# The expert layers of a two-layer encoder step: rows of the first two experts gathered by a 0/1 product, ranks in four products, weight slots reassigned, expert rows moved to other queues

## The chip, the cores and the metric

One core of one Trainium2 chip. The metric is the device time of one execution in microseconds (us). TensorE does matmuls, VectorE (DVE) and ScalarE (ACT) elementwise work, GpSimd (POOL) mostly issues DMAs here, SyncE (SP) only issues DMAs. Each engine runs its own instruction list in order and meets the others at semaphores. All DMA queues are served by the core's 16 DMA engines.

## The reference

Two layers over 384 tokens (256 of a prompt, 128 of eight samples), each with a mixer and a mixture of experts. Layer 0 mixes with a chunked gated MLP, layer 1 with latent attention. The part that the change touches is the mixture of experts and what stands right before and after it:

```python
t = xn.reshape(-1, D_MODEL)                    # 384 x 1024, after an RMS norm
lg = tf @ w_group + b_group                    # 4 groups, top 1
le = (tf @ w_expert + b_expert)                # 16 experts, 4 in a group
top_v, top_i = lax.top_k(le_sel, 2)            # top 2 in the chosen group
wts = softmax(top_v) * g_p
for e in range(16):                            # only the routed tokens count
    hdn = silu(t @ w1[e]) * (t @ w3[e])        # 1024 -> 512
    y = y + gates[:, e:e+1] * (hdn @ w2[e])    # 512 -> 1024
```

## The kernel before, in words

All products with large weights are done in three passes of the reduced-precision float type: the weight is split on ACT into a high part (`moe_split_h`, line 1028) and on DVE into the rest (`moe_split_l`, line 1032), and x likewise. One expert weight is 2 MB and has the number j = 0 to 47 in a layer: j = 0, 1 are w1 and w3 of expert 0, 2 and 3 those of expert 1, 4 is w2 of expert 0, 5 is w1 of expert 2, and from there w1[e] is 3e-1, w3[e] is 3e and w2[e] is 3e+4 (the last w2 is 47). TensorE does product j from bank to bank in this order and counts `w_used`. "Product j" below is the 24 matmuls of 512 columns of one weight (lines 181 and 187).

Six slots hold raw weights, six the low parts, three the high ones (w_hi). Six weights are loaded ahead of the loop, and load j waits until product j-6 is done. In layer 0 the slots 2 to 5 are free before the output product of the gated MLP ends, the slots 0 and 1 only near its end; before the change expert 0's w1 and w3 sit in slots 0 and 1.

Routing of a layer (`route_tensor`, `route_scalar`, `route_vector`): the mixer's last product ends; DVE adds it to h and multiplies by the gain for each of three row tiles (lines 378 and 878 in layer 0, 1483 and 878 in layer 1); TensorE transposes each tile (line 996), ACT copies it, TensorE computes the logits (line 1003). ACT takes the square root of the mean squares, DVE scales the rows (885) and then does a chain of small operations, each waiting for the last: logits (889), group, two experts per token, the matrix `picked` of 0 and 1. TensorE ranks the tokens of each expert with nine products against a triangle and a block of ones (1016). DVE turns ranks into destination rows (910 to 927). POOL scatters the normed rows to `moe_xrows` in DRAM, six indirect DMAs (849). When they have landed, SP loads the 72 rows of experts 0 and 1 (744), TensorE transposes them (1156), ACT and DVE split them (`x_high` 1044, `x_low` 1102), and product 0 starts. After `x_low(0)` DVE builds the table of overfull experts (941 to 961), used by a loop of ten conditional steps on SP, ACT, DVE and TensorE at the layer's end. No expert ran over in this profile.

The expert loop in steady state: TensorE does product 3e-1, the transposes of the hidden rows of e-1, product 3e, the transposes of x of e+1, product 3e+1. ACT does silu, hidden, three splits, `x_high`, and `y_copy` (1055) of e-1; DVE the matching low parts and the gated hidden. SP's list is: load w1[e], load x rows e (744), load w3[e], load w2[e-1], store y rows of e-4 (751). A store waits until the store before it has landed, as the regions overlap; `y_copy(e)` waits until the store of e-2 has landed.

At a layer's end SP stores y of expert 15, in layer 0 then issues the loads of the attention's w_uk and cached rows (1336 to 1342), waits for the last store, runs the loop of ten conditional steps, and signals `y_final` (819), on which POOL gathers the y rows back (854) and DVE combines them into h. TensorE starts the attention's key work (1714) when w_uk and the cache are there.

## Time and profile before

| | us |
|---|---|
| median of 3 runs (lowest, highest) | 1226.12 (1221.96, 1231.62) |
| the profiled execution: device time | 1225.43 |
| its span from first to last instruction | 1223.6 |
| busy TensorE / DVE / ACT / POOL | 1031.5 / 776.7 / 594.6 / 52.1 |
| mean granted TensorE clock, share of 2.4 GHz | 0.916 |

The profiled execution lies 0.7 us below the median, and 1.8 us of it lie outside the span. Layer 0's gated MLP ends at about 234 us, its routing lasts until 297, its experts until 588; the attention lasts until 855, the second routing until 908, the second experts until 1195. In the two routing stretches TensorE is mostly idle and at half its clock; in the two expert stretches it is busy all the time.

### The profile page before, as it was taken

The page shows a single profiled execution, that of the slowest core. Times are in us where ns is not written, and L with a number is a line of the kernel's source. Part 1 is how long each engine was busy: PE and PEld are TensorE (multiplying, and loading weights), DVE is VectorE, ACT ScalarE, POOL GpSimd, SP SyncE. Part 2 cuts the span into 40 slices and gives each one's busy share as a digit, 9 for nine tenths or more (in the row PEclk, how much of TensorE's full clock was granted, in tenths as well). Part 3 has the DMA queues.
Part 4 walks back from the last instruction along what each step waited for, and adds up shares of the span by engine and source line. Part 5 has one row for each costly group of instructions (what it writes and reads, how often), then busy time and mean ns, then how long its engine had stood idle before and what let it go on. Part 6 is the DMA issues. An engine that isn't in the chain of part 4 may idle for free.

```text
span 1223.6 us, 13100 instructions
## 1 busy us (share of the span) xinstructions
PE 1031.5 (84%) x4905; PEld 741.5 (61%) x4905; DVE 776.7 (63%) x605; ACT 594.6 (49%) x451; POOL 52.1 (4%) x72
## 2 busy tenths in 40 slices
PE   5999999663899999999498867688638999999990
PEld 4889988561566666665375736564525666666650
DVE  4547561363688898888144653653627888888862
ACT  5236432151577777766132323132415777777750
POOL 4000000003000000000210100000010000000001
PEclk9999999955899999999699986899569999999995
DMA  9524315703799999994560103006147999999934
GB/s 340 167 100 182 143 69 232 317 18 140 277 377 385 377 383 389 381 377 188 178 214 1 32 1 138 0 1 281 63 146 301 384 394 382 384 391 391 381 130 164
DMA packets 44823, 281.39 MB, mean 230 GB/s; under 512 B 6000, under 2 KB 10384, under 8 KB 32096
## 3 DMA queue, kind: packets, MB, share of 16 engines
q1 hardware_dynamic: 38512, 259.05, 55.7%
q0 software_dynamic: 6272, 21.81, 5.3%
q8 instruction: 26, 0.43, 0.1%
q14 instruction: 13, 0.11, 0.0%
HBM read 262.05 MB, written 19.09 MB: 230 GB/s over the span
## 4 chain that ended last, share of the span: by engine, by line
PE 51%; issue 28%; DMA 8%; DVE 7%; ACT 4%; POOL 1%; SPq 0%; POOLq 0%; ACTq 0%; DVEq 0%
PE ps L181 11%; PE ps L187 5%; DMA moe_yrows<-moe_rows 4%; PE ps L516 4%; PE ps L570 4%; PE ps L613 3%; PE ps L1750 2%; PE ps L1776 2%; PE ps L576 2%; PE ps L524 2%; PE ps L1910 2%; PE ps L1003 2%; DMA raw<-in_moe_w_dram 1%; PE ps L620 1%; POOL moe_xrows L849 1%
## 5 line engine op out<-in xcount | busy, mean ns | idle before, releaser
L1032 DVE TENSOR_TENSOR raw_lo<-raw,moe_wh 128x4096 fp32r<-128x4096 f32 x48 | 212.4, 4425 | 57.2 <-ACT moe_wh L1028 57.0
L1032 DVE TENSOR_TENSOR moe_wl<-moe_raw,moe_wh 128x4096 fp32r<-128x4096 f32 x48 | 212.3, 4424 | 50.1 <-ACT moe_wh L1028 50.0
L181 PE MATMUL ps<-moe_wh,moe_xh 128*72 128x512 f32 x512 | 207.7, 406 | 13.0 <-DVE moe_xl L1102 13.0
L181 PE MATMUL ps<-moe_wh,moe_xl 128*72 128x512 f32 x512 | 205.1, 401 | 0.0
L1028 ACT ACTIVATE moe_wh<-raw 128x4096 fp32r<-128x4096 f32 x48 | 173.8, 3622 | 32.2 <-DMA raw<-in_moe_w_dram 28.3
L1028 ACT ACTIVATE moe_wh<-moe_raw 128x4096 fp32r<-128x4096 f32 x48 | 173.8, 3622 | 4.1 <-DMA moe_raw<-in_moe_w_dram 4.1
L181 PEld LDWEIGHTS ps<-moe_wh,moe_xh 128*72 128x72 f32 x512 | 74.5, 145 | 59.8 <-DVE moe_xl L1102 13.6
L181 PEld LDWEIGHTS ps<-moe_wh,moe_xl 128*72 128x72 f32 x512 | 74.5, 146 | 43.9 <-issue 3.2
L321 DVE TENSOR_TENSOR raw_lo<-raw,gm_wh 128x4096 fp32r<-128x4096 f32 x12 | 53.1, 4426 | 70.5 <-ACT gm_wh L315 68.1
L181 PE MATMUL ps<-moe_wh,moe_hTh 128*72 128x512 f32 x256 | 81.3, 399 | 3.4 <-DVE moe_hTl L1107 3.3
L181 PE MATMUL ps<-moe_wh,moe_hTl 128*72 128x512 f32 x256 | 79.6, 392 | 0.0
L1044 ACT ACTIVATE moe_xh<-ps 128x576 fp32r<-128x576 f32 x32 | 20.9, 652 | 103.9 <-PE ps L1156 103.8
L187 PE MATMUL ps<-raw_lo,moe_xh 128*72 128x512 f32 x272 | 68.5, 394 | 0.0
L315 ACT ACTIVATE gm_wh<-raw 128x4096 fp32r<-128x4096 f32 x11 | 39.9, 3627 | 58.6 <-DMA raw<-in_gm_w_in_dram 29.8
L1055 ACT ACTIVATE moe_rows<-ps 72x1024 f32<-72x1024 f32 x32 | 32.7, 1022 | 69.2 <-PE ps L187 60.6
L187 PE MATMUL ps<-moe_wl,moe_xh 128*72 128x512 f32 x240 | 60.6, 394 | 0.0
L1156 PE MATMUL ps<-const,moe_rows 72*128 72x72 f32 x256 | 22.5, 233 | 42.2 <-DMA moe_rows<-moe_xrows 42.2
L187 PEld LDWEIGHTS ps<-raw_lo,moe_xh 128*72 128x72 f32 x272 | 38.4, 141 | 24.2
L1156 PEld LDWEIGHTS ps<-const,moe_rows 72*128 72x128 f32 x256 | 21.8, 146 | 47.9 <-DMA moe_rows<-moe_xrows 42.4
L181 PEld LDWEIGHTS ps<-moe_wh,moe_hTl 128*72 128x72 f32 x256 | 36.3, 142 | 22.9
L516 PE MATMUL ps<-gm_wh,gm_fx 128*128 128x512 f32 x192 | 46.3, 402 | 2.9 <-ACT gm_wh L308 2.9
L187 PEld LDWEIGHTS ps<-moe_wl,moe_xh 128*72 128x72 f32 x240 | 33.9, 141 | 21.7
(345 smaller groups left out, 1547.2 us busy)
## 6 DMA issues: line engine op xcount, KB each, us to landing
raw<-in_moe_w_dram SPq DMA_DIRECT2D x48, 2048.0 KB, 11.6
moe_raw<-in_moe_w_dram SPq DMA_DIRECT2D x48, 2048.0 KB, 12.6
raw<-in_gm_w_in_dram SPq DMA_DIRECT2D x7, 2048.0 KB, 8.1
moe_rows<-moe_xrows SPq DMA_DIRECT2D x32, 288.0 KB
moe_yrows<-moe_rows SPq DMA_DIRECT2D x32, 288.0 KB
raw<-in_gm_w_out_dram SPq DMA_DIRECT2D x4, 2048.0 KB, 7.4
raw<-in_gm_w_in_dram SPq DMA_DIRECT2D x2, 1024.0 KB, 11.7
at_cache<-in_cache_ckv_dram SPq DMA_DIRECT2D x2, 1024.0 KB, 11.4
```

What stands on the lines that cost most here:

```text
L181: nc.tensor.matmul(out[c], x(t, k), wh[:, k, c * 512:c * 512 + 512], start=start and k == 0 and x is xh, stop=False)
L187: last = nc.tensor.matmul(out[c], xh(t, k), wl[:, k, c * 512:c * 512 + 512], start=False, stop=stop and k == nk - 1)
L315: nc.scalar.activation(w_gm[s][:], raw[:, s, :], ACT.Copy).then_inc(wh_ready, 1)
L321: nc.vector.tensor_tensor(raw_lo[:, s, :], raw[:, s, :], w_gm[s][:].bitcast(F32), ALU.subtract).then_inc(wl_ready, 1)
L516: nc.tensor.matmul(ps[:, 3 * (m % 2) + t], x_rows(x, k, t), wh[:, k], start=k == 0 and x is xth, stop=False)
L524: last = nc.tensor.matmul(ps[:, 3 * (m % 2) + t], x_rows(xth, k, t), wl[:, k], start=False, stop=k == KD - 1)
L570: nc.tensor.matmul(ps[:, u_bank(c), 0:TOK], wh[:, k, i * P:(i + 1) * P], x[:, k], start=k == 0 and x is xth, stop=False)
L613: nc.tensor.matmul(ps[:, 2 * t + c], x_rows(x, 4 * j + k, t), wh[:, k, c * 512:c * 512 + 512], start=j == 0 and k == 0 and x is uth, stop= ...
L1028: nc.scalar.activation(w_hi[hi][:], w_raw[slot], ACT.Copy).then_inc(wh_ready, 1)
L1032: nc.vector.tensor_tensor(w_lo[slot], w_raw[slot], w_hi[hi][:].bitcast(F32), ALU.subtract).then_inc(wl_ready, 1)
L1055: nc.scalar.activation(rows[0:CAP, 2 + par].rearrange("p (b n) -> p b n", b=2), ps[0:CAP, BY:BY + 2], ACT.Copy).then_inc(y_out, 1)
L1156: last = nc.tensor.transpose(ps[:, BX + k // 4, (k % 4) * CAP:(k % 4 + 1) * CAP], rows[0:CAP, par, k * P:(k + 1) * P], ident[0:CAP, 0:CAP])
```

## The change

Eight parts, none of which changes a result:

1. **Slots by layer** (`SLOT`). In layer 0 the weights j = 0 to 3 go to slots 2 to 5, which are free early, and j = 4 and 5 to slots 0 and 1. In layer 1 j = 2 goes to slot 4 and j = 5 to the slot that is free last.
2. **Tile by tile after the attention.** TensorE signals `at_y` after each row tile of the output product and DVE adds tile t when it is there; before, it waited for all three. ACT squares tiles 0 and 1 before its first copy.
3. **Routing.** Two small DVE operations of the chain go or move behind `picked`; the ranks take four products of up to 64 columns in the reduced type (nine in full type before); the low part that DVE did between `picked` and the ranks moves behind `x_low(0)`, ahead of the table: in layer 0 low parts 1 and 2, in layer 1 low part 2.
4. **Experts 0 and 1 from SBUF.** DVE writes a 0/1 matrix `hot` (128 x 3 x 72) for each of the two, by comparing rank + 1 with 1 to 72; TensorE multiplies the row tiles with it: 8 x 3 matmuls of 72 columns for each expert, in place of the load and eight transposes. The scatter stays, for experts 2 to 15.
5. **x rows of experts 2 to 15** are loaded by POOL's queue, one as soon as TensorE has transposed the rows two experts before.
6. **y rows** are stored by ACT's queue: the store of e-1 stands behind the third split of step e; the last two stand behind `y_copy(14)` (ahead of `hidden_high(15)`) and behind `y_copy(15)`.
7. **The end of a layer.** SP runs the loop of ten conditional steps while the last products still run and waits for the last store after it. In layer 0 SP loads the cache when product 46 is done and w_uk when product 47 is.
8. ACT makes a reduced-type copy of the triangle and the ones at the start; the constants have 72 more columns; the attention's oT lies elsewhere in SBUF.

```diff
+        SLOT = [[2, 3, 4, 5, 0, 1], [0, 3, 4, 5, 1, 2]]
@@ moe_sync, layer 0 (load(name, expert, j, slot))
                 sp.wait_ge(utl_ready, PAIRS)
-                load("moe_w1", 1, 2, 2)
-                load("moe_w3", 1, 3, 3)
+                load("moe_w1", 0, 0, S[0])
+                load("moe_w3", 0, 1, S[1])
                 sp.wait_ge(stored, V_STORED)
-                load("moe_w2", 0, 4, 4)
-                load("moe_w1", 2, 5, 5)
+                load("moe_w1", 1, 2, S[2])
+                load("moe_w3", 1, 3, S[3])
                 sp.wait_ge(w_used, m0 - 1)
-                load("moe_w1", 0, 0, 0)
+                load("moe_w2", 0, 4, S[4])
                 sp.wait_ge(w_used, m0)
-                load("moe_w3", 0, 1, 1)
+                load("moe_w1", 2, 5, S[5])
@@ moe_sync, end of a layer
+                    sp.wait_ge(y_stored, 16 * (E0 + NE))      # inside the If of an overfull expert
+                    sp.wait_ge(w_used, m0 + 3 * NE)
...
+            if l == 0:
+                load_cache(sp)                                # w_used 47: cache; w_used 48: w_uk
             at_least(sp, s["st"], 16 * n_over + 16)
+            sp.wait_ge(y_stored, 16 * (E0 + NE))
             sp.sem_inc(y_final, 1)
@@ moe_pool
+            def load_x(e, par):
+                row = g.value_load(first_i[0:1, bass.ds(e, 1)], min_val=0, max_val=SLOTS)
+                g.wait_ge(xT_done, NE * l + (2 if isinstance(e, int) and e == 2 else e - 1))
+                g.dma_start(rows[0:CAP, par, :], xrows[bass.ds(row, CAP), :]).then_inc(x_loaded[par], 16)
@@ route_vector
             dve_link(v, nc.vector.tensor_tensor(lem4, le.rearrange("p t (g j) -> p t g j", g=NG),
-                                                gsel[:].unsqueeze(3).to_broadcast(shape4), ALU.mult))
-            dve_link(v, nc.vector.tensor_tensor(lem4, lem4, pen[:].unsqueeze(3).to_broadcast(shape4), ALU.add))
+                                                pen[:].unsqueeze(3).to_broadcast(shape4), ALU.add))
...
-            moe_split_l(v, l, *([1, 1, 1] if l == 0 else [2, 2, 2]))
             v.wait_ge(rt_rank, l + 1)
             dve_link(v, nc.vector.tensor_copy(rank[:], ps[:, BR, 128:192].rearrange("p (t e) -> p t e", e=NE)))
+            dve_link(v, nc.vector.scalar_tensor_tensor(spot[:], rank[:, 0:TILES], 1.0, picked[:, 0:TILES].bitcast(F32),
+                                                       ALU.add, ALU.mult))
+            expert_hot(v, 0)
...
+        def expert_hot(v, e):
+            shape = [P, TILES, CAP]
+            nc.vector.tensor_tensor(hot[:, e], const[:, C_SLOT:C_SLOT + CAP].unsqueeze(1).to_broadcast(shape),
+                                    spot[:, :, e].unsqueeze(2).to_broadcast(shape), ALU.is_equal).then_inc(rt_hot, 1)
@@ route_tensor
+            for s in range(TILES + 1):
+                if s == 0:
+                    last = nc.tensor.matmul(ps[:, BR, 128:192], sums[:, 0:P], picked[:], start=True, stop=False)
+                else:
+                    last = nc.tensor.matmul(ps[:, BR, 128 + s * NE:192], sums[:, P:], picked[:, 0:TILES + 1 - s], start=False,
+                                            stop=s == TILES)
@@ moe_scalar, in a step, behind the third split (and behind y_copy in the last step and after it)
+            def store_y(e, par):
+                row = a.value_load(first_i[0:1, bass.ds(e, 1)], min_val=0, max_val=SLOTS)
+                at_least(a, y_stored, 16 * (E0 + e))
+                a.wait_ge(y_out, E0 + e + 1)
+                a.dma_start(yrows[bass.ds(row, CAP), :], rows[0:CAP, 2 + par, :]).then_inc(y_stored, 16)
@@ moe_vector
             x_low(0, 0)
+            if l == 0:
+                moe_split_l(v, 0, 1, 1, 1)
+            moe_split_l(v, l, 2, 2, 2)
             table_vector(v)
@@ moe_tensor
-            transpose_x(0, 0)
+            def gather_x(e):
+                pe.wait_ge(rt_hot, 2 * l + e + 1)
+                at_least(pe, xl_ready, E0 + e)
+                for k in range(KD):
+                    for t in range(TILES):
+                        last = nc.tensor.matmul(ps[:, BX + k // 4, (k % 4) * CAP:(k % 4 + 1) * CAP], rows[:, t, k * P:(k + 1) * P],
+                                                hot[:, e, t], start=t == 0, stop=t == TILES - 1)
+                last.then_inc(xT_done, 1)
+            gather_x(0)
@@ a step: behind product 1
-                if not is_last(e):
+                if f:
+                    gather_x(1)
+                elif not is_last(e):
                     transpose_x(e + 1, 1 - par)
@@ at_vector
-            v.wait_ge(at_y, 1)
             v.wait_ge(stored, LAT_STORED)
             for t in range(TILES):
+                v.wait_ge(at_y, t + 1)
```

## Rows read from the trace of the kernel before

**Rows 1.** Window in layer 0's expert loop: length, busy per engine, granted clock, DMA share, GB/s.

```profile
350.00:500.00 150.00, 150.00 (x723) 94.41 (x722) 131.63 (x52) 113.48 (x62) 0.00 (x0) 1.00 1.00 383
```

**Rows 2.** Chain that ended last, layer 0: start us, us, what.

```profile
217.28 16.68 DMA raw<-in_moe_w_dram
233.98 3.63 ACT moe_wh L1028
237.63 4.42 DVE raw_lo L1032
243.29 2.04 DVE moe_rows L878
...
255.55 6.66 PE ps L1003 x32
268.00 4.33 DVE raw_lo L1032
...
297.49 5.30 PE ps L181 x16
...
314.95 6.68 PE ps L181 x16
...
323.75 3.72 PE ps L181 x16
...
510.85 17.82 DMA moe_yrows<-moe_rows
```

**Rows 3.** Window behind the last product of the gated MLP, columns as above.

```profile
236.00:240.00 4.00, 0.00 (x0) 0.00 (x0) 2.37 (x1) 1.59 (x1) 0.00 (x0) 0.89 0.89 381
```

**Rows 4.** Timeline of routing, layer 0: start, us, engine, line, what, idle before.

```profile
232.45 2.01 PE L620 MATMUL ps<-raw_lo,gm_uth 128*128 128x512 f32 x8
...
262.33 0.79 DVE L889 SCALAR_TENSOR_TENSOR rt_logit<-ps,stat,broute 128x20 f32<-128x20 f32 x3 [1.49 <-PE ps L1003]
...
267.98 4.03 PE L1016 MATMUL ps<-rt_picked,const 128*128 128x16 f32 x18 [5.78 <-DVE rt_picked L905]
...
277.73 4.38 POOL L849 DMA_INDIRECT moe_xrows<-moe_rows,rt_dst_i  x1 [0.30 <-issue]
...
302.39 0.17 DVE L961 CAST rt_over_table_i<-rt_over_table 1x21 int32<-1x21 f32 x1
```

**Rows 5.** Window of layer 1's logits, instructions of line 1003 alone: PE, PEld, clock.

```profile
862.00:874.00 12.00, 8.77 (x42) 9.08 (x42) 0.50 0.01 2
```

**Rows 6.** Timeline from the attention's end into layer 1's experts.

```profile
829.02 3.84 PE L1901 MATMUL ps<-at_pcT,raw 128*128 128x128 f32 x32 [0.47 <-ACT at_pcT L1663]
...
834.45 20.84 PE L1910 MATMUL ps<-raw,at_oT 128*128 128x512 f32 x48 [1.59 <-DVE at_oT L1477]
...
875.68 0.79 DVE L889 SCALAR_TENSOR_TENSOR rt_logit<-ps,stat,broute 128x20 f32<-128x20 f32 x3 [1.27 <-PE ps L1003]
...
906.04 0.65 ACT L1044 ACTIVATE moe_xh<-ps 128x576 fp32r<-128x576 f32 x1 [24.45 <-PE ps L1156]
...
906.79 0.76 DVE L1102 TENSOR_TENSOR moe_xl<-ps,moe_xh 128x576 fp32r<-128x576 f32 x1 [16.65 <-ACT moe_xh L1044]
```

**Rows 7.** Timeline of the ends of both layers' experts.

```profile
588.30 1.02 ACT L1055 ACTIVATE moe_rows<-ps 72x1024 f32<-72x1024 f32 x1 [6.37 <-PE ps L187]
...
599.40 3.62 PE L1714 MATMUL ps<-const,at_w_uk 128*64 128x128 f32 x16 [11.14 <-DMA at_cache<-in_cache_krope_dram]
...
1196.43 0.33 SPq L751 DMA_DIRECT2D moe_yrows<-moe_rows  x1
...
1205.46 0.98 POOL L854 DMA_INDIRECT moe_rows<-moe_yrows,rt_dst_i  x1 [308.37 <-SPq L819]
```

**Rows 8.** SP's instructions of line 805, behind the last store: shortest/median/longest ns, first, last.

```profile
L805 SPq TENSOR_LOAD <-rt_over_table_i x2: 436/437/438, 592.7 to 1199.4; - x2
```

**Rows 9.** ACT's timeline in layer 1's loop: where its idle time lies.

```profile
984.98 0.59 ACT L1063 ACTIVATE moe_silu<-ps 72x512 f32<-72x512 f32 x1 [0.99 <-PE ps L187]
```

**Rows 10.** Group of the y copies on ACT: busy, mean ns, idle before, by releaser.

```profile
L1055 ACT ACTIVATE moe_rows<-ps 72x1024 f32<-72x1024 f32 x32 | 32.7, 1022 | 69.2 <-PE ps L187 60.6 <-DMA moe_yrows<-moe_rows 8.6
```

More of the change, by code:

```diff
@@ L675, in build @@
         wts = sb("rt_weight", [P, 2, TILES], F32, moe)
-        picked = sb("rt_picked", [P, TILES, NE], F32, moe)
+        picked = sb("rt_picked", [P, TILES + 1, NE], F32R, moe)
+        spot = sb("rt_spot", [P, TILES, NE], F32, moe)
+        both = sb("rt_both", [P, 2, TILES, NE], F32, moe)
         rank = sb("rt_rank", [P, TILES + 1, NE], F32, moe)
@@ L679, in build @@
         first = sb("rt_first", [P, 2 * NE], F32, moe)
-        dst = sb("rt_dst", [P, TILES, 2], F32, moe)
+        dst = sb("rt_dst", [P, 2 * TILES], F32, moe)
         dst_i = sb("rt_dst_i", [P, TILES * 2], U32, moe)
         first_i = sb("rt_first_i", [P, NE], I32, moe)
-        squares_junk = sb("rt_squares", [P, D], F32, moe)
+        with ExitStack() as before:
+            squares_junk = sb("rt_squares", [P, D], F32, before)
+        hot = sb("rt_hot", [P, 2, TILES, CAP], F32, moe)
         ov = sb("rt_over", [P, 4, NE], F32, moe)
@@ L789, in moe_sync @@
+                load("moe_w3", e, 3 * e, S[3 if par else 0])
+                load("moe_w2", e - 1, 3 * e + 1, S[4 if par else 1])
             for e in range(2, 5):
@@ L1013, in route_tensor, with moe_split_h @@
             pe.wait_ge(rt_picked, 2 * l + 1)
-            for t in range(TILES + 1):
-                for s in range(min(t + 1, TILES)):
-                    last = nc.tensor.matmul(ps[:, BR, 128 + t * NE:128 + (t + 1) * NE], upper if s == t else ones,
-                                            picked[:, s], start=s == 0, stop=s == min(t, TILES - 1))
+            for s in range(TILES + 1):
[4 more added lines that the diff above has]
+                                            stop=s == TILES)
             last.then_inc(rt_rank, 1)
-        def moe_split_h(a, l, j, hi, slot, q):
+        def moe_split_h(a, l, j, hi, r, q):
+            slot = SLOT[l][r]
             a.wait_ge(raw_loaded[slot], 16 * raw_count(l, slot, q))
@@ L1911, in at_tensor @@
                                                 w_o[:, k, c * 512:c * 512 + 512], start=k == 0, stop=k == 3)
-            last.then_inc(at_y, 1)
+                last.then_inc(at_y, 1)
         def expand(pe):
```

154 lines of the change are left out of this document (76 added, 78 removed).

## The prediction

> **What bounds the kernel now.** I read the windows first. In the expert loops TensorE is busy for 150.00 of 150 us at full clock, and the DMA share is 1.00 [rows 1]. One expert is three products: 16 matmuls in 3.7 us (at 323.75 in [rows 2]) and eight more at the same pace in 1.85, so 5.55 each, and with the transposes 17.4. There nothing can be gained but by fewer TensorE instructions, and the change removes none. The time that is open lies between the loops. In layer 0 TensorE ends the mixer at 232.45 + 2.01 = 234.46 [rows 4] and starts product 0 at 297.49 [rows 2]: 63.0 us. In layer 1 it ends at 834.45 + 20.84 = 855.29 and starts at 907.6, behind `x_low` at 906.79 + 0.76 [rows 6]: 52.3 us. Then come two ends: from the last product of layer 0 (588.3) to the attention's first work at 599.40, 11.1 us, and from the last product of layer 1 (1196.43 less 1.2) to POOL's gather at 1205.46, 10.2 us [rows 7]. The chain of waits [rows 2] tells what stands in layer 0's hole: a DMA, a split, a low part, logits at half speed, another low part, the scatter and reload.
>
> **From the mixer to the logits, layer 0.** w1 of expert 0 is issued only at 217.28 and lands at 233.96; ACT and DVE need 3.63 and 4.42, and DVE's add for tile 0 waits behind them until 242 [rows 2]. With slot 2, issued first some 16 us earlier, the weight is there when `w_used` allows the split, at 217.3 (the same count released the load at 217.28). Split to 220.9, low part to 225.4. An add takes 1.24 (243.29 less 237.63 + 4.42) and a gain product 2.04: tiles 0 and 1 are ready before TensorE is, tile 2 at 234.5 + 3.3 = 237.8. TensorE then does 3 x 8 transposes and 3 x 16 logit records. At half clock the logits take 6.66 / 32 = 0.208 us a record [rows 2], so 3.3 a tile; the transposes about 1.9 a tile. At full clock, by the 0.12 of a 128-column record of line 1901 [rows 6], 1.9 and 1.0. After 234.5 the clock stayed full for most of 5 us (mean 0.89 in 236 to 240 [rows 3]). So I take transposes 0, 1, logits 0 and transposes 2 at full, two logits at half: 234.5 + 1.0 + 1.0 + 1.9 + 1.2 + 6.7, with waits 246.7. DVE's own chain (copy, root, row scaling) needs 5.3 behind the last transposes, to 245. Before, the chain began at 262.33 [rows 4]: gain 15.6, bounds 12.0 (all at half) and 17.3 (DVE's chain last).
>
> **The same in layer 1.** With `at_y` by tile only tile 2 is left when the product ends: its rows at 855.3 + 3.3 = 858.6. By the same sum the logits end at 867.4; before 875.68 [rows 6]: gain 8.3, bounds 4.5 and 10.7.
>
> **Picks and ranks, each layer.** Of the 5.65 us from 262.33 to 267.98 two links of 0.22 go. 18 rank records took 4.03 us, and DVE was busy with a low part until 272.33 [rows 2, 4]. Four records: about 1.0, and no low part ahead of the copy. 4.35 becomes 1.1. Gain 0.45 + 3.25 = 3.7, bounds 3.3 and 3.9.
>
> **Rows of experts 0 and 1.** From the copy of the ranks to product 0 it took 297.49 - 272.33 = 25.2 in layer 0, and 907.6 - 885.7 = 21.9 in layer 1 (its chain runs 10.0 us like layer 0's). The difference is one scatter that took 4.38 us [rows 4] while DVE ran the low part that began at 276.82. After: copy, `spot`, `hot` (each 0.25 to 0.35) 0.85; then 24 full-type matmuls, 48 records. They have the logits' weights, 128 x 128, and more columns, 72 against 20; at half clock I take the logits' pace: 48 x 0.21 = 10.2. `x_high` 0.65 and `x_low` 0.76 with their hand-overs 1.5 [rows 6]. Together 12.6. Gain 12.5 and 9.3. The other bound is the pace of line 1901, 48 x 0.12 = 5.8: 4.4 more in each. What hides the scatter now: it must end before POOL loads expert 2's rows, needed some 30 us later.
>
> Clock, weighed with a rule: 42 records of logits within 12 us, back to back, did not lift the clock from 0.50 [rows 5], so I leave the gather at half. The Trainium skill (TensorE: Matmul & The Clock Gate, Part 1) says that the default is the throttled state and sustained matmul activity releases it. By it the back-to-back gather would mostly run at full clock, and the sum would be the first rival's; these logits do not agree.
>
> **From product 0 to product 2.** Before: 314.95 - 297.49 = 17.5 in layer 0 [rows 2], and I take the same in layer 1. This start now has more on DVE. Layer 0: low parts 1 and 2 (4.42 each), table (302.56 - 297.4 = 5.2 [rows 4]), low part 3 4.42, hidden 1.07, `x_low(1)` 0.76: 20.4. TensorE is back earlier: 7.2 for product 0 (half speed at first), 5.55, gather(1) 5.8, 1.5 for the splits: 20.0. So 20.4, a loss of 2.9. Layer 1 has one low part less on DVE, so TensorE decides, 19.5: loss 2.0. Product 2 then starts at half speed again, 6.68 against 3.72 [rows 2], as before. At product 2 the lead is 15.6 + 3.7 + 12.5 - 2.9 = 28.9 in layer 0, 8.3 + 3.7 + 9.3 - 2.0 = 19.3 in layer 1.
>
> **The loop.** ACT gets a store in each step: a register load 0.44 [rows 8], checks, the issue 0.33 [rows 7], some 1.3 in all. It stands before silu, where ACT is idle for 0.99 [rows 9]; 0.3 is left over, and DVE's idle time ahead of the next product's needs is above that. Cost 0. POOL's x loads have an expert's time, 17.4 us. SP loses only waits. A gain is possible where a y copy waited for a store: 8.6 us on ACT [rows 10], in layer 0's last steps, of which TensorE lost 0 to 2.6. I take 1.5.
>
> The Trainium skill (SBUF — State Buffer, "Who interferes with whom") says that a DVE operation with two SBUF inputs blocks a GpSimd instruction that reads SBUF. That speaks against POOL as the x queue; the 4.38 us scatter agrees. Its price here would be one low part per load, all hidden within 17.4 us; on the path it adds nothing.
>
> **The ends.** The store of 14 now stands ahead of `hidden_high(15)`, on the path to product 47: between 0.5 (issue alone) and 1.3; 0.9 in each layer, loss 1.8. Layer 0: the cache is issued 7.7 us before the last product ends, w_uk at its end, so they land some 4 us behind it; but TensorE must first get through its own ten conditional steps. SP's run from 1199.4 to the signal at 1205.2, 5.8 [rows 8, 7]. So TensorE starts 5.8 behind the last product in place of 11.1: gain 5.3, bounds 3 (loads late) and 7. The y gather comes earlier too but stays behind the key work. Layer 1: the ten steps (5.8) leave the path between store and `y_final`, ACT's register load may add 0.6: gain 5.6, bounds 5 and 5.8.
>
> **Sum.** 28.9 + 19.3 + 1.5 - 1.8 + 5.3 + 5.6 = 58.8. Against the profiled 1225.4: 1166.6, say 1167 (the median lies 0.7 higher, which is nothing). The copy at the start hides behind the first transposes; the 37 KB of constants cost 0.1.
>
> **Rivals.** (a) The gather lifts or holds the clock. It saves 4.4 in each layer, product 0's slow start in layer 1 (1.6; in layer 0 DVE ends last), product 2's in both (3.0 each), and some 4 in the logits: 20 in all, 1147. For: products lift it within a few us. Against: rows 5. (b) The lead is partly lost: logits all at half (3.6 + 3.8), loads at the turn late (2.3), the last steps as before (1.5): 1178. It is the slow end of the same forecast. (c) Slower: the y store on ACT. If its landing stays as slow as the 17.82 us on SP's queue [rows 2] and more, ACT waits at the next store with three splits queued behind it, and an expert takes landing + 0.7. This costs from a landing of 16.7 us on; at 18.8 it has eaten the 59 (2.1 x 28 experts), at 20 it gives 1167 + 28 x 3.3 = 1259. For it: the DMA share is 1.00. Against: that store stood behind two weights of 2 MB in one queue, which it leaves. (d) The gain of the gather does not come, as experts 2 and 3 wait for the scatter instead: their rows are needed 17 us behind gather(1) at best; if they came 10 late in each layer, 1187.
>
> **Chances.** Forecast, (b) included, 0.66; (a) 0.22; (d) 0.06; (c) 0.04; something that makes no difference of it all 0.02. Range: from 1147 to 1184. A measurement here tells 1% from no change (12 us). Faster 0.94, same 0.02, slower 0.04.
>
> **What would show it.** In the new profile: the add of tile 0 before 230 and DVE's line of logits at 247; four rank records in 1 us; 48 gather records in 10 us at clock 0.50, product 0 at 266 in layer 0; product 2 20 us later; DVE without a gap before `x_low(1)` in layer 0; no ACT wait for y stores; TensorE's key work 6 us behind product 47; `y_final` 4 us behind the last y copy. The prediction is wrong if the loop's 17.4 us an expert changes, since 0.5 us there is 14 us, or if the clock is another in the two routings.

## The result, and the profile after

The changed kernel takes 1165.7 us (median of 4 runs, 1164.5 to 1167.1), the kernel before 1228.9 beside it (1222.0 to 1239.5). The ratio is 0.948, with a 95% interval of 0.941 to 0.955. The forecast was 1167 (1147 to 1184). The profiled execution took 1164.5, its span is 1162.9, and the granted clock is 0.942 of full (0.916 before).

The span can be cut at marks that every kernel here has: the first line of logits on VectorE, the starts of products 0, 2 and 3 (written #3), the y copies of experts 14 and 15, the attention's key work, its output product. Each cell is the distance to the mark before it, read from the timelines.

| stretch (us) | before | after | gained | forecast |
|---|---|---|---|---|
| start to logits, layer 0 | 262.3 | 243.8 | 18.5 | 15.6 |
| logits to product 0 | 35.2 | 19.3 | 15.9 | 3.7 + 12.5 |
| product 0 to product 2 | 17.5 | 20.0 | -2.5 | -2.9 |
| product 2 to #3 | 8.6 | 7.4 | 1.2 | 0 |
| #3 to y copy 14 | 257.1 | 255.2 | 1.9 | 1.5 |
| y copy 14 to y copy 15 | 7.7 | 8.6 | -0.9 | -0.9 |
| to the key work | 11.1 | 4.1 | 7.0 | 5.3 |
| attention, to its output product | 235.1 | 236.3 | -1.2 | 0 |
| output product | 20.8 | 20.8 | 0 | 0 |
| to the logits, layer 1 | 20.4 | 13.2 | 7.2 | 8.3 |
| logits to product 0 | 31.9 | 19.3 | 12.6 | 3.7 + 9.3 |
| product 0 to product 2 | 17.8 | 19.4 | -1.6 | -2.0 |
| product 2 to #3 | 7.3 | 7.4 | -0.1 | 0 |
| #3 to y copy 14 | 254.8 | 255.2 | -0.4 | 0 |
| y copy 14 to y copy 15 | 7.7 | 10.1 | -2.4 | -0.9 |
| to the end | 28.4 | 22.8 | 5.6 | 5.6 |

The gains add to 60.8, and the spans differ by 60.7 (1223.6 less 1162.9). The forecast column adds to 58.8. The forecast started from the profiled 1225.4 of before; by the medians the gain is 63.2.

**From the mixer to product 2, layer 0.** This is the chain of waits after, with start, duration and what, and answers to [rows 2] and [rows 4]:

```profile
231.57 1.86 PE ps L626 x8
233.43 0.89 PE ps L1004 x8
...
235.49 1.96 PE ps L1011 x16
237.45 0.92 PE ps L1004 x8
238.36 5.31 PE ps L1011 x32
...
243.79 0.25 DVE rt_logit L891
...
248.99 0.42 PE ps L1024
249.41 0.61 PE ps L1026 x3
...
250.99 10.53 PE ps L1215 x48
...
262.29 0.77 DVE moe_xl L1127
...
263.11 5.71 PE ps L184 x16
...
276.23 5.33 PE ps L1215 x48
...
283.07 5.50 PE ps L184 x16
```

The DMA, the split and the two low parts of [rows 2] are gone from the chain. The logits end 10.4 us behind the mixer's product (233.43 to 243.8) where it took 27.9. The first logits (line 1011) run at full clock, 16 records in 1.96; the other two tiles take 5.31. Four rank records take 1.0. Then comes the product with the 0/1 matrix (line 1215), 48 records in 10.53, and the same 48 in 5.33 for expert 1.

The windows after, columns as in [rows 1], say at which clock. The first answers to [rows 3], the last to [rows 1]:

```profile
236.00:240.00 4.00, 4.00 (x37) 4.00 (x37) 0.76 (x1) 2.91 (x5) 0.53 (x1) 0.97 0.94 402
240.00:244.00 4.00, 3.66 (x18) 3.54 (x17) 2.64 (x5) 3.99 (x3) 0.00 (x0) 0.50 0.35 134
...
350.00:500.00 150.00, 150.00 (x723) 94.19 (x722) 131.62 (x53) 113.29 (x61) 4.30 (x9) 1.00 1.00 392
```

The clock falls from full (2.4 GHz) to half (1.2 GHz) just before 240, with TensorE busy all of the time. It stays there through the first product of rows; the second runs between products 1 and 2 at full clock. The loop is what it was: TensorE busy in 150.00 of 150 us at clock 1.00.

**ScalarE in the loop.** Its timeline after, over one step, which answers to [rows 9] and [rows 10]:

```profile
528.71 1.03 ACT L1069 ACTIVATE moe_rows<-ps 72x1024 f32<-72x1024 f32 x1 [1.37 <-PE ps L190]
529.63 3.62 ACT L1039 ACTIVATE moe_wh<-raw 128x4096 fp32r<-128x4096 f32 x1
529.94 0.54 ACTq L1077 DMA_DIRECT2D moe_yrows<-moe_rows  x1
```

The store is issued at 529.94, while the split of 529.63 is still running: its 0.54 lies beside the engine's work and does not lengthen it. The group of all y copies after shows no wait for a store any more:

```profile
L1069 ACT ACTIVATE moe_rows<-ps 72x1024 f32<-72x1024 f32 x32 | 32.7, 1023 | 67.4 <-PE ps L190 67.4
```

**The ends.** This is the timeline after at the end of layer 0, then of layer 1. It answers to [rows 7]:

```profile
545.64 0.39 SPq L1376 DMA_DIRECT2D at_cache<-in_cache_ckv_dram  x1
...
547.47 0.41 ACT L1060 ACTIVATE moe_hTh<-ps 128x288 fp32r<-128x288 f32 x1 [0.80 <-ACT moe_rows L1069]
...
554.24 0.37 SPq L1385 DMA_DIRECT2D at_w_uk<-in_w_uk_dram  x1
...
558.37 1.91 PE L1757 MATMUL ps<-const,at_w_uk 128*64 128x128 f32 x8 [4.16 <-DMA at_w_uk<-in_w_uk_dram]
...
1132.75 0.69 PE L184 MATMUL ps<-moe_wh,moe_hTh 128*72 128x512 f32 x2 [2.56 <-DVE moe_hTl L1132]
...
1140.13 1.02 ACT L1069 ACTIVATE moe_rows<-ps 72x1024 f32<-72x1024 f32 x1 [7.92 <-PE ps L190]
1141.36 0.54 ACTq L1077 DMA_DIRECT2D moe_yrows<-moe_rows  x1
1144.58 1.01 POOL L856 DMA_INDIRECT moe_rows<-moe_yrows,rt_dst_i  x1 [70.77 <-SPq L808]
```

The key work waits for w_uk alone, 4.1 us behind its issue; TensorE's own ten conditional steps lie within that. In layer 1 the y gather starts 4.5 behind the last product, in place of 10.2. In front of the last product (first row of layer 1) stands the new pause: `hidden_high(15)` comes 0.80 late, and TensorE idles 2.56.

### The profile page after: what moved, and what is told of

Read it like the earlier page. It is cut to its first block, busy times and chain, and to the rows that moved or that the text cites. A ratio compares the mean times of both kernels' runs of the same rounds, so it can differ in the third digit from the quotient of the medians.

```text
span 1162.9 us, 13401 instructions
## 1 busy us (share of the span) xinstructions
PE 1044.8 (90%) x5037; PEld 753.9 (65%) x5037; DVE 777.8 (67%) x605; ACT 594.9 (51%) x453; POOL 63.6 (5%) x101
## 4 chain that ended last, share of the span: by engine, by line
PE 84%; DVE 6%; ACT 5%; DMA 3%; issue 2%; POOL 0%; ACTq 0%; POOLq 0%; SPq 0%; DVEq 0%
PE ps L184 31%; PE ps L190 15%; PE ps L522 4%; PE ps L576 4%; PE ps L619 3%; PE ps L1215 3%; PE ps L1819 3%; PE ps L1793 2%; PE ps L582 2%; PE ps L530 2%; PE ps L626 1%; PE ps L1184 1%; PE ps L1841 1%; PE ps L1935 1%; PE ps L1011 1%
## 5 line engine op out<-in xcount | busy, mean ns | idle before, releaser
L190 PE MATMUL ps<-moe_wl,moe_xh 128*72 128x512 f32 x272 | 68.6, 394 | 0.0
L1056 ACT ACTIVATE moe_xh<-ps 128x576 fp32r<-128x576 f32 x32 | 20.9, 652 | 87.7 <-PE ps L1184 52.9
L190 PE MATMUL ps<-raw_lo,moe_xh 128*72 128x512 f32 x240 | 60.6, 394 | 0.0
L190 PEld LDWEIGHTS ps<-moe_wl,moe_xh 128*72 128x72 f32 x272 | 38.4, 141 | 24.6
L184 PEld LDWEIGHTS ps<-moe_wh,moe_hTh 128*72 128x72 f32 x256 | 34.3, 143 | 23.3 <-DVE moe_hTl L1132 5.4
L522 PE MATMUL ps<-gm_wh,gm_fx 128*128 128x512 f32 x192 | 46.1, 400 | 2.9 <-ACT gm_wh L311 2.9
L190 PEld LDWEIGHTS ps<-raw_lo,moe_xh 128*72 128x72 f32 x240 | 33.9, 141 | 21.6
L576 PE MATMUL ps<-gm_fx,gm_wh 128*128 128x384 f32 x256 | 45.2, 335 | 0.0
## 6 DMA issues: line engine op xcount, KB each, us to landing
at_cache<-in_cache_ckv_dram SPq DMA_DIRECT2D x2, 1024.0 KB, 10.4
```

The lines of the kernel that those rows point to most:

```text
L184: nc.tensor.matmul(out[c], x(t, k), wh[:, k, c * 512:c * 512 + 512], start=start and k == 0 and x is xh, stop=False)
L190: last = nc.tensor.matmul(out[c], xh(t, k), wl[:, k, c * 512:c * 512 + 512], start=False, stop=stop and k == nk - 1)
L522: nc.tensor.matmul(ps[:, 3 * (m % 2) + t], x_rows(x, k, t), wh[:, k], start=k == 0 and x is xth, stop=False)
L576: nc.tensor.matmul(ps[:, u_bank(c), 0:TOK], wh[:, k, i * P:(i + 1) * P], x[:, k], start=k == 0 and x is xth, stop=False)
```

## The experiments

All are the changed kernel (1165.7) with one edit each, unless said otherwise. The ratios are to the kernel before, measured beside each group of runs. Its median was 1229.2 beside the first four, 1234.3 beside last store, filler, one gather and low part between, and 1228.2 beside the others; the changed kernel was timed beside 1228.9 alone. So a difference of medians from 1165.7 holds to some 5 us, and the readings rest on the stretches. The table gives those that the edits touch, from the profiled execution of each; "rest" is what else differs by over 1 us. The first number of a pair is of layer 0, the second of layer 1.

| run | median | logits to product 0 | 0 to 2 | copy 14 to 15 | attention | rest |
|---|---|---|---|---|---|---|
| changed kernel | 1165.7 | 19.3, 19.3 | 20.0, 19.4 | 8.6, 10.1 | 236.3 | |
| rows loaded | 1188.1 | 29.0, 28.8 | 19.9, 18.9 | 8.6, 8.6 | 242.3 | 2 to #3: 8.6, 8.1; logits in layer 1: 11.0 |
| slots as before | 1183.9 | 19.3, 19.2 | 20.4, 19.4 | 10.2, 10.1 | 237.5 | start to logits: 262.2; 2 to #3: 5.9, 7.4 |
| one signal | 1177.6 | 19.3, 19.3 | 20.2, 19.7 | 10.1, 8.6 | 242.8 | logits in layer 1: 20.5; 2 to #3: 5.9, 7.4 |
| ends as before | 1174.3 | 19.3, 19.3 | 20.3, 19.6 | 10.1, 10.1 | 234.9 | to the key work 9.5; end 28.7; 2 to #3: 5.9, 7.4 |
| last store late | 1160.5 | 19.3, 19.3 | 20.7, 20.9 | 7.7, 7.7 | 236.0 | start to logits: 245.0; 2 to #3: 5.8, 5.8 |
| filler | 1168.2 | 19.3, 18.9 | 20.8, 20.4 | 10.2, 10.1 | 242.2 | logits in layer 1: 10.5; 2 to #3: 5.8, 5.8 |
| one gather | 1153.5 | 18.6, 17.6 | 11.2, 12.7 | 10.1, 10.2 | 242.4 | 2 to #3: 5.8, 5.8; logits in layer 1: 11.0 |
| y on SyncE | 1174.8 | 19.3, 19.3 | 20.5, 20.1 | 7.7, 7.7 | 236.0 | start to logits: 244.8; to the key work 15.3; end 26.4; 2 to #3: 5.8, 5.8; logits in layer 1: 10.7 |
| low part between | 1174.7 | 22.7, 22.7 | 20.4, 20.1 | 10.1, 10.2 | 241.2 | start to logits: 246.9; 2 to #3: 5.9, 5.9; logits in layer 1: 10.7 |
| both | 1138.1 | 17.5, 17.1 | 12.8, 12.7 | 7.7, 7.7 | 235.8 | logits in layer 1: 10.3; 2 to #3: 5.8, 5.8 |
| both, filler | 1136.9 | 16.8, 16.8 | 12.7, 12.7 | 7.7, 7.7 | 235.6 | logits in layer 1: 10.3; 2 to #3: 5.8, 5.8 |
| both, attention | 1138.1 | 17.5, 17.4 | 12.8, 12.8 | 7.7, 7.7 | 235.3 | logits in layer 1: 10.3; 2 to #3: 5.8, 5.8 |

In all of them #3 to y copy 14 takes 255.1 to 255.2, in both layers. "2 to #3" has two lengths in most runs, 5.8 and 7.4, by whether the clock falls in product 2; where it is 5.8, "0 to 2" is 0.2 to 1.6 longer than in the changed kernel, except in the runs with one product of rows.

**Rows loaded.** The rows of experts 0 and 1 come out of DRAM again.

```diff
-            gather_x(0)
+            transpose_x(0, 0)
...
-                if f:
-                    gather_x(1)
-                elif not is_last(e):
+                if not is_last(e):
...
-            for e in range(2, 4):
+            for e in range(4):
                 load_x(e, e % 2)
```

> The changed kernel (1165.7), with the rows of experts 0 and 1 scattered, loaded back and transposed again (two loads more on GpSimd's queue, no product with the 0/1 matrix). My theory: in the trace of the changed kernel product 0 starts 13.1 us behind the copy of the ranks in both layers; the way through DRAM takes 21.9 where no low part runs beside the scatter, so +8.8 in each. Of this the second product of rows (5.5 us on TensorE) comes back only where VectorE allows it: nothing in layer 0, where its queue ends at the same time (product 2 behind product 0 by 20), 3.4 in layer 1 (16 in place of 19.4). Sum +14.2: 1180 (1176 to 1184). Rival, the prediction's own terms: 12.5 and 9.3, less a loss of 2.9 and 2.0: +16.9, 1182.6. Rival two: the gather's gain is all there and its cost is none: +21.8, 1187.5. Told apart by where product 0 and product 2 start.

Measured: 1188.1, ratio 0.964 (0.957 to 0.971), +22.4. From the logits to #3 layer 0 takes 57.5 in place of 46.7, layer 1 55.7 in place of 46.1: the product with the 0/1 matrix is worth 10.8 and 9.6 where it stands. Another 6.0 is the attention's, whose instructions the edit doesn't touch (below). The late product 0 was right (+9.7, +9.4 against +8.8). What missed is layer 1's product 2, expected at 16 and found at 18.9. These rows of this run's timeline (ScalarE, then VectorE) say why:

```profile
879.85 1.28 ACT L1085 ACT_TABLE_LOAD   x1 [8.29 <-PE ps L190]
881.15 0.59 ACT L1085 ACTIVATE moe_silu<-ps 72x512 f32<-72x512 f32 x1
881.64 3.61 ACT L1040 ACTIVATE moe_wh<-moe_raw 128x4096 fp32r<-128x4096 f32 x1
...
885.29 4.42 DVE L1045 TENSOR_TENSOR moe_wl<-moe_raw,moe_wh 128x4096 fp32r<-128x4096 f32 x1 [3.41 <-ACT moe_wh L1040]
```

The split of weight 3 waits for silu and its table load; its low part, 3.41 idle before it, stands ahead of hidden and `x_low(1)`. So between product 0 and product 2 there is a third chain, through ScalarE, that is hardly shorter than the other two (18.9 against 19.4). With VectorE idle the six issues of the scatter take 0.95 to 1.02 each; before, one took 4.38 beside a low part [rows 4]. The Trainium skill (SBUF — State Buffer, "Who interferes with whom") says that a VectorE instruction with two SBUF inputs contends with a GpSimd instruction that reads SBUF, and both traces agree.

**Slots as before.** `SLOT[0]` is the identity, and w1 of expert 0 is loaded last.

```diff
-        SLOT = [[2, 3, 4, 5, 0, 1], [0, 3, 4, 5, 1, 2]]
+        SLOT = [[0, 1, 2, 3, 4, 5], [0, 3, 4, 5, 1, 2]]
...
-                load("moe_w1", 0, 0, S[0])
-                load("moe_w3", 0, 1, S[1])
-                sp.wait_ge(stored, V_STORED)
                 load("moe_w1", 1, 2, S[2])
...
+                load("moe_w1", 0, 0, S[0])
```

> The changed kernel (1165.7), with layer 0's six first weights in the slots and the order of loading of before, so that w1 of expert 0 comes last. My theory: VectorE's line of logits goes back from 10.8 to 27.9 us behind the mixer's last product, +17.1: 1182.8 (1180 to 1185). Rival: logits at half clock would hide a part of the late weight, +12.0 (the prediction's low bound): 1177.7. Rival two: nothing, as the clock or DMA that is freed gives it back: 1166.

Measured: 1183.9, ratio 0.961 (0.954 to 0.968), +18.2. The logits start at 262.2 in place of 243.8, and nothing downstream gives it back. Its row is that of before [rows 4], 0.1 us earlier:

```profile
262.21 0.79 DVE L891 SCALAR_TENSOR_TENSOR rt_logit<-ps,stat,broute 128x20 f32<-128x20 f32 x3 [1.49 <-PE ps L1011]
```

**One signal.** All three adds of layer 1 wait for the whole output product.

```diff
-                v.wait_ge(at_y, t + 1)
+                v.wait_ge(at_y, TILES)
```

> The changed kernel (1165.7), in which layer 1's adds all wait for the last tile of the output product. My theory: logits on VectorE go back from 13.2 to 20.35 us behind the product, +7.1: 1172.8. Rival: only the adds and gain products of two tiles move (2 x 3.3 = 6.6), and TensorE's clock is full for the first logits, so +5: 1170.7. A third: the change of clock decides and it costs under 3: 1168.

Measured: 1177.6, ratio 0.955 (0.948 to 0.963), +11.9, beyond all three. The stretch that the edit touches did what the first theory said, 20.5 in place of 13.2, +7.3. The largest other difference is the attention ahead of it: 242.8 in place of 236.3, though nothing is changed there. This is a window of the changed kernel:

```profile
738.00:758.00 20.00, 11.52 (x62) 9.92 (x62) 12.79 (x23) 4.60 (x9) 0.00 (x0) 0.91 0.00 1
```

And this is the same window of this run, whose key work starts within 0.4 us of the other's:

```profile
738.00:758.00 20.00, 11.42 (x39) 9.26 (x40) 12.26 (x19) 3.13 (x5) 0.00 (x0) 0.68 0.00 1
```

The granted clock is 0.91 in one and 0.68 in the other, and TensorE gets through 62 instructions against 39 in the same 11.5 busy us. Up to about 134 us behind the key work the two traces run within 0.6 of each other; VectorE's instructions of the slower one lie 1.0 behind at 166 us and 6.5 behind at 199, so the difference arises in this stretch. A low clock there isn't all of it: the run "both" below has 0.67 over the same stretch and still takes 235.8, as it was 2.4 ahead of the changed kernel at 166 us and lost 3.2 by 199.

**Ends as before.** SyncE waits for the last y copy, loads for the attention then, waits for the last store and only then takes the ten conditional steps.

```diff
             s = over[l]
+            if l == 0:
+                sp.wait_ge(y_out, E0 + NE)
+                load_cache(sp)
+            sp.wait_ge(y_stored, 16 * (E0 + NE))
             sp.wait_ge(rt_table, l + 1)
...
```

> The changed kernel (1165.7), with the ends of the two layers as before: SyncE waits for the last y copy, issues the loads for the attention (w_uk first, then the cache; layer 0 alone), waits for the last store to land and only then goes through its ten conditional steps. My theory: in layer 0 TensorE's key work starts 11.1 us behind the last product in place of 4.1, +7.0; in layer 1 the y gather starts 10.2 behind in place of 4.5, +5.7: sum +12.7, 1178.4. Rival: layer 0 gains from something else (the gather of y, the conditional steps of TensorE) and only layer 1 comes back: +5.7, 1171.4.

Measured: 1174.3, ratio 0.953 (0.946 to 0.960), +8.6. Layer 1's end grows by 5.9 (28.7), where 5.7 was expected. The key work comes 9.5 behind the last product and not 11.1, so layer 0 gives 5.4 of the expected 7.0; it waits for the cache, issued 1.5 to 2.0 us behind the product. The attention is 1.4 shorter here.

**Last store late.** The store of expert 14 goes behind `hidden_high(15)`.

```diff
                 if is_last(e):
                     y_copy(e - 1, 1 - par)
-                    store_y(e - 1, 1 - par)
                     return
...
             hidden_high(NE - 1)
+            store_y(NE - 2, 0)
             y_copy(NE - 1, 1)
```

> The changed kernel (1165.7), with the store of expert 14's rows issued behind hidden_high(15) on ScalarE instead of ahead of it. My theory: from the y copy of 14 to the last product's end it takes 8.6 us in layer 0 and 10.15 in layer 1 (before the change 7.7 in both). The store itself is 0.8 of it; the other 1.6 in layer 1 is TensorE's clock, which falls in the longer pause (2.56 us in place of 1.64), so that the last product runs 7.35 in place of 5.77. Without the store ahead both are gone: -0.9 and -2.4, 1162.4. Rival: only the issue counts, the clock falls anyway: -1.7, 1164.0.

Measured: 1160.5, ratio 0.938 (0.933 to 0.944), -5.2. Both layers are back at 7.7. The row of the last product in layer 1 reads:

```profile
1131.22 0.68 PE L184 MATMUL ps<-moe_wh,moe_hTh 128*72 128x512 f32 x2 [1.65 <-DVE moe_hTl L1132]
```

The pause is 1.65 in place of 2.56, and the product takes 5.8 in place of 7.35. Over all traces this stretch has three lengths. Without the store ahead (the kernel before and five runs, two layers each) it is 7.7 twelve times in twelve. With it, it is 8.6 four times (the store's 0.9) and 10.1 twelve times (and half clock in the product). So the longer pause does not always cost the clock, but mostly. In the four cases of 8.6 the pause is 2.56 as well. The mechanism is the theory's. The two last products give 0.9 and 2.4, and the spans of the two profiled executions differ by no more than these 3.3 (1162.9 and 1159.6); the other 1.9 of the -5.2 lies between medians and is shown by no trace.

**Filler.** Twenty wide matmuls behind the logits and two ahead of the first product of rows, whose results nobody reads.

```diff
+                nc.tensor.matmul(ps[0:CAP, 6, 0:2 * P], sums[:, 0:CAP], sums[:], start=True, stop=True)
...
             logits(2)
+            keep_busy(20)
             pe.wait_ge(rt_picked, 2 * l + 1)
```

> The changed kernel (1165.7) with added work that nobody reads: 20 matmuls of 256 columns behind the logits, while VectorE picks, and two ahead of the first product with the 0/1 matrix. It asks whether TensorE's clock can be had for the first product of rows (10.5 us at 0.50; the second takes 5.5 at 1.00). My theory: wide matmuls lift it where narrow ones of full type did not: -5.0 for the rows, -1.6 for product 0's slow start, in each layer: -13, 1153. Rival: the clock stays at 0.50 through them, as it did in 12 us of logits: 1166. Rival two: it rises in them but falls again within the narrow matmuls (the clock fell within the logits after a wide product at full clock): half of it, -5, 1160.

Measured: 1168.2, ratio 0.944 (0.938 to 0.950); the product of rows takes 10.51. Windows from the fillers on:

```profile
244.00:248.00 4.00, 2.30 (x14) 2.05 (x12) 3.41 (x18) 4.00 (x2) 0.00 (x0) 0.81 0.00 0
248.00:252.00 4.00, 2.13 (x9) 1.75 (x9) 2.79 (x15) 2.12 (x3) 0.00 (x0) 0.62 0.00 0
252.00:256.00 4.00, 4.00 (x21) 4.00 (x20) 2.73 (x15) 0.00 (x0) 1.25 (x2) 0.50 0.00 0
```

The clock did rise (mean 0.81 in the first window), and was at half again when the product began; it then stayed at 0.50 with TensorE busy for all of it. In layer 1 it was full until the product began (839.5), and the product took 10.52 all the same. So the first theory falls, and the half gain of rival two doesn't come either.

**One gather.** The rows of both experts in one product, its result in banks 0, 1 and 5; both splits ahead of the loop; one low part in VectorE's idle time; hidden ahead of the low part of weight 3.

```diff
+                        last = nc.tensor.matmul(ps[:, (BX, BX + 1, BY)[k // 3], (k % 3) * 2 * CAP:(k % 3 + 1) * 2 * CAP],
+                                                rows[:, t, k * P:(k + 1) * P], hot[:, :, t], start=t == 0, stop=t == TILES - 1)
+                last.then_inc(xT_done, 2)
...
+            moe_split_l(v, l, *([1, 1, 1] if l == 0 else [2, 2, 2]))
             x_low(0, 0)
+            x_low(1, 1)
```

> The changed kernel (1165.7), with the rows of experts 0 and 1 made in one product (24 matmuls of 144 columns in place of twice 24 of 72), both splits ahead of the loop, one low part while VectorE waits for the product, and hidden ahead of the low part of weight 3. My theory: a record of 72 columns takes 0.219 at half clock, one of the logits with 20 columns 0.208, so it is the 128 x 128 weight that costs and not the columns: the product for both takes 11 to 12. Then product 2 follows product 1 without a hole: from product 0 to product 2 13 in place of 20.0 and 19.4, and its slow start (1.8 to 3) goes too; of that up to 1 goes to the longer first product. -7 in each layer: 1151.5 (1147 to 1157). Rival: columns cost, the product takes twice as long (20): the gain is 7 - 9.5, 1170. Rival two: what is won is lost at the first loads of the loop, which come no earlier: 1160.

Measured: 1153.5, ratio 0.934 (0.928 to 0.939), -12.2. The timeline of TensorE in this run:

```profile
251.29 9.18 PE L1239 MATMUL ps<-rt_hot,moe_rows 128*128 128x144 f32 x48 [1.27 <-DVE rt_hot L942]
262.39 0.45 PE L184 MATMUL ps<-moe_wh,moe_xh 128*72 128x512 f32 x1 [1.93 <-DVE moe_xl L1146]
```

And three windows of it:

```profile
252.00:256.00 4.00, 4.00 (x18) 4.00 (x18) 3.59 (x15) 0.00 (x0) 1.38 (x2) 0.50 0.03 12
256.00:260.00 4.00, 4.00 (x28) 4.00 (x28) 3.15 (x1) 0.00 (x0) 4.00 (x1) 0.81 0.31 121
260.00:264.00 4.00, 2.07 (x11) 1.30 (x11) 1.56 (x4) 1.64 (x4) 2.87 (x4) 1.00 0.81 315
```

Twice the rows take less time than half of them did: 9.18 against 10.52. In the window at half clock (252 to 256) the pace is 18 records, 0.22 each, as with 72 columns, so columns cost nothing there. Then, unlike in the narrow product, the clock rises within it, 6.2 us behind its start here and 4.1 in layer 1. Product 2 follows 11.2 and 12.7 behind product 0. From the logits to #3 it is 35.6 and 36.1, in place of 46.7 and 46.1: -21.1. No run parts the one product from the three changes of order that came with it. The spans differ by 15.8 only: the attention took 6.1 more and layer 0's last product 1.5, and the logits of layer 1 gave 2.1. The other three executions were 4 to 8 us longer than the profiled one.

**Y on SyncE.** The stores of the y rows go back between the weight loads.

```diff
                 load("moe_w2", e - 1, 3 * e + 1, S[4 if par else 1])
+                if not (isinstance(e, int) and e < 4):
+                    store_y(e - 4, par)
...
+            for e in range(NE - 4, NE):
+                store_y(e, e % 2)
...
```

> The changed kernel (1165.7), with the stores of the y rows back on SyncE's queue, three experts late and between its weight loads, as before. It asks what the move to ScalarE was worth. My theory: in layer 0 the stall of the last experts returns (product 2 to the last product 273.3 before, 271.2 after, of which the last product's late start hides 1 to 2.5): +2 to +3; layer 1 has none. The last products start without the store ahead of them: -0.9 and -2.4. The ends grow, since SyncE's ten conditional steps stand behind the last store again: +2.7 in layer 1, and in layer 0, where the attention's loads stand behind them too, +7. Sum +9: 1174.5. Rival: the store on ScalarE costs time in each expert (the third rival of the prediction in small), so that the loop gets faster: below 270 in both layers, 1168. Rival two: the loop with stores between the loads is slower in all experts, by 0.1 each, +3 more in either layer: 1180.

Measured: 1174.8, ratio 0.957 (0.952 to 0.961), +9.1. The total fits the theory, but not by its parts. The loop's stall does not come back: #3 to y copy 14 is 255.2, and no y copy waits for a store. The end of layer 0 costs 11.2 and not 7, as SyncE issues the attention's loads only at 560.95, behind its ten conditional steps and 6.4 behind the last store (before, they stood ahead of the steps):

```profile
560.95 0.42 SPq L1385 DMA_DIRECT2D at_cache<-in_cache_ckv_dram  x1
```

The end of layer 1 costs 3.6. Both last products gain what they should. So the 1.9 us that the change won in layer 0's loop isn't the place of the stores alone. It isn't the slots and the order of the first weights alone either: with those as before, #3 to y copy 14 is 255.1. The x loads on SyncE, or two of the three together, remain, and no run here tries them.

**Low part between.** One low part back between picks and ranks, as before.

```diff
+            moe_split_l(v, l, *([1, 1, 1] if l == 0 else [2, 2, 2]))
             v.wait_ge(rt_rank, l + 1)
```

> The changed kernel (1165.7), with one low part of a weight (4.4 us on VectorE) back between the picks and the copy of the ranks, where it stood before; it no longer stands behind x_low(0). My theory: product 0 starts 3.4 later in each layer (4.4 less the 1.0 in which the copy waited for the ranks anyway); from product 0 to product 2 TensorE decides and gives nothing back: +6.8, 1172.5. Rival: VectorE decides there, as the prediction has it for layer 0, and a low part less behind x_low(0) gives 3 back: +3.8, 1169.5.

Measured: 1174.7, ratio 0.950 (0.945 to 0.956), +9.0. Product 0 comes 3.4 later in both layers, and product 2 gives nothing back (20.4, 20.1): the theory's +6.8. From product 0 to #3 it is 26.2 and 26.0, within what the other runs with two products of rows have (26.1 to 27.4 and 26.0 to 27.1, rows loaded apart). The rest is an earlier stretch (+3.1 ahead of the logits) and the attention (+4.9) less what other stretches give. The rows of products 0 and 2 in layer 0 read:

```profile
269.63 0.70 PE L184 MATMUL ps<-moe_wh,moe_xh 128*72 128x512 f32 x1 [1.60 <-DVE moe_xl L1128]
...
290.00 0.46 PE L184 MATMUL ps<-moe_wh,moe_xh 128*72 128x512 f32 x1 [1.53 <-DVE moe_xl L1128]
```

**Both.** One gather and the last store late.

> One product for the rows of experts 0 and 1 (1153.5 alone) and the store of 14 behind hidden_high(15) (1160.5 alone, 5.2 under the changed kernel). My theory: in the run with one product the last product still ended 10.1 us behind #46 in both layers, and 7.7 is what it takes without the store: -4.8, 1148.7. Rival: the gain of the last store came from the attention's clock, which lay at its better end in that run: -1.7, 1151.8.

Measured: 1138.1 (6 runs, 1136.7 to 1143.6), ratio 0.928 (0.924 to 0.931), where 1148.7 was expected. The last products take 7.7 each in place of 10.1, which is the theory's 4.8. The rest of the miss isn't the edit's. The attention is 235.8 in this profile and was 242.4 in that of one gather; and the sum was made from that run's median, 1153.5, while its profiled execution took 1148.75. What made its other executions longer is in no trace. By spans "both" is 26.7 us below the changed kernel: 21.2 of it between the logits and #3 of the two layers, 3.4 at the last products, and 2.9 as the logits of layer 1 come sooner; the other stretches cost 0.8 together.

**Both, filler**, with 24 and six unread matmuls around the ranks, and **both, attention**, with 24 of them in TensorE's 5.6 us wait for `at_work`:

```diff
+                if t == 1:
+                    pe.wait_ge(at_PTc, 1)
+                    keep_busy(24, 4)
                 pe.wait_ge(at_p2, t + 1)
```

> The kernel of the run before (expected at 1148.7) with 24 wide matmuls behind the logits and six ahead of the product of rows, all unread. With 72 columns the clock of 0.8 that such matmuls had brought was lost again within the product; with 144 it rises from 0.50 to 1.00 within the product by itself, 5 to 6 us in. My theory: with 144 columns the raised clock is kept, the product takes 6.5 in place of 9.2 and 8.1: -4.5, 1144. Rival: it falls in the pause of the picks (3 us) and nothing is left of it: 1148.7.

> The kernel with both edits (expected at 1148.7), with 24 wide unread matmuls in the attention, in the 5.6 us in which TensorE waits for VectorE's at_work. Without them the stretch from the key work to the output product takes 235 to 243 us in the traces so far, with the same instructions and a clock of 0.67 to 0.91 in the 20 us behind that pause. My theory: that spread is TensorE's clock, decided in this pause; the matmuls hold it, 235 to 237 us in every run, and the median falls by up to 6: 1144. Rival: the level is set before the pause, and the stretch stays at 241 to 243 where it was: 1149.

Measured: 1136.9, ratio 0.927 (0.923 to 0.930), and 1138.1, ratio 0.928 (0.925 to 0.932). With the first filler the product of rows takes 7.82 in place of 8.05, and product 0 starts 0.7 and 0.3 earlier: neither 4.5 nor nothing, and too little to keep. The second changes nothing that can be measured. Its attention is at 235.3, but so it is without it (235.8), and its six times still fall in two groups (1137.6, 1137.7, 1138.0, 1138.1 and 1143.3, 1146.2), as do those of "both" (1136.7 to 1138.2 and 1143.3, 1143.6). So filling the pause at `at_work` doesn't remove the spread. What the longer executions have isn't plainly a lower mean clock: the filler run's 1146.1 was granted 0.957 as its others were (0.955 to 0.957), and of the four longer ones of "both" and "both, attention" only one (1143.6, at 0.949) lies below the short ones (0.952 to 0.954).

## Why the prediction was right

**The logits of layer 0** start 17.5 earlier behind the mixer (10.4 in place of 27.9) where 15.6 was taken, and this is the upper bound, 17.3: the first tile's logits and the last transposes ran at full clock, so TensorE's logits end together with VectorE's row scaling, at 243.7. Another 1.0 came before the mixer's end. Undone, the step costs 18.4. **In layer 1** it is 7.2 against 8.3, because the clock fell already in the last tile's transposes; undone, 7.3. When it falls varies with nothing changed there: 4.4 to 4.5 behind the product in the changed kernel and three other runs, whose logits start 12.7 to 13.2 behind it, and 5.6 to 7.9 behind it in eight runs, whose logits start at 10.3 to 11.0, near the upper bound.

**Picks, ranks and rows** gave 15.9 and 12.6 against 16.2 and 13.0. The product of rows was taken at 10.2 at half clock and took 10.52. A low part between picks and ranks costs 3.4, which is the row's 3.25 for ranks and copy.

**Product 0 to product 2** lost 2.5 and 1.6 against 2.9 and 2.0. The prediction let VectorE decide in layer 0 at 20.4 and TensorE come to 20.0; it was 20.0. The run with the low part between shows that TensorE decides in both layers: that low part was taken out of VectorE's queue there, and it changed nothing. In layer 0 it is a near thing in the changed kernel: VectorE is done with hidden at 282.15 and ScalarE with `x_high(1)` at 282.23. That product 2 would start at half speed was right only in part (5.50 in place of 6.68).

**The loop** gained 1.9 where 1.5 was taken, but the reason given, stores that wait on SyncE, isn't supported: with the stores back there it stays gained. So that the term fits is luck as far as is known. ScalarE's store costs nothing, as forecast, and even less than argued, since it is issued beside a running split. Rival (c) had nothing to it, and neither had (d): the load of expert 2's rows is issued at 282.3, and their transposition at 296.25 stands in the chain without a wait.

**The last products** are the term that is furthest off for its size, 1.8 taken and 3.3 measured: 0.9 in each layer was right for the store, but the longer pause also cost the clock, 1.5 more in layer 1 (and in 12 of 16 cases over all traces). The prediction had no term for that.

**The ends** gave 7.0 and 5.6 against 5.3 and 5.6. TensorE's conditional steps, which I took for the bound in layer 0 at 5.8, are through in under 4.1; w_uk is what it waits for, and it lands the 4 us behind the last product that the prediction gave for it.

**The sum** hides these misses. The start to the logits of layer 0 gave 2.9 more than taken, its end 1.7 and the clock in its product 2 1.2 more; the last product of layer 1 took 1.5 more, its logits gave 1.1 less and the attention 1.2 less. That 58.8 met 60.7 so closely is in part that they cancel; the two large terms, the logits of layer 0 and the way from the logits to product 0, were each right by themselves.

**Rival (a)**, a clock that the rows' product lifts, did not occur with this product, and did with one of twice the columns: in all eight products of 144 columns that the four traces show, in none of the sixteen first products of 72. The Trainium skill (TensorE: Matmul & The Clock Gate, Part 1) has sustained matmul work release the throttle; TensorE was busy without a gap for 10.5 us at 0.50 in one kernel and rose in the other, so being busy alone, in these traces, did not do it.

## What to carry to other kernels

Where a small gather costs its weights and not its columns, put everything that shares the weights into one product; here that removed the second product and part of the slow clock, and with the order of splits changed beside it gave 21 us. Ahead of a short last piece of work, look at what each engine issues before the instruction on the path: 0.8 us of store cost 2.4 in layer 1 through the clock. Compare variants by stretches cut at marks, since one untouched stretch moved by 8 us here, as much as several of the edits were worth.

## What the runs showed of the hardware

- The attention's 235 us vary between 234.9 and 242.8 over fourteen traces with the same instructions (24 unread matmuls more in one); in the pair compared above the difference arises where the clock is 0.91 in one and 0.68 in the other. What sets the level isn't settled, and "both" took 235.8 with 0.67 there.
- A DMA issued on ScalarE's queue takes 0.54 us there, and it overlaps the activation that is running (529.94 within 529.63 to 533.25).
- Full-type matmuls with 128 x 128 weights take 0.22 us a record at half clock with 20, 72 and 144 columns alike; the product with 72 kept the clock at 0.50 for all of its 10.5 us, in 16 of 16 cases. In the one with 144 it went to 1.00 in 8 of 8 cases, 3.2 to 6.2 us behind the product's start. The second product of 72 columns, which follows product 1 at full clock, kept full clock for its 5.5 us in 16 of 16.
- After a pause of 1.65 us the last product ran at full clock to its end (5.8 us), after one of 2.56 it fell to half within it (7.35). With the longer pause it fell in 12 of 16 cases, with the shorter in none of 12.
